# Where a fused attention kernel sums the squares of its input rows: on ScalarE beside the first projection, or on VectorE between the pieces that the projection waits for

## The chip, the cores and the metric

The kernel runs on one core of a Trainium2 chip. The metric is the device time of one execution in microseconds. Profiles are of one execution; their span runs from the first to the last instruction.

## The reference

Two transformer mixers follow each other over an input of 512 rows and 2048 columns, then a final norm. What the change touches is the beginning of the first:

```python
def rms_norm(x, g):
    y = xf * lax.rsqrt(jnp.mean(xf * xf, axis=-1, keepdims=True) + RMS_EPS)
    return y * g

h = rms_norm(x, swa_norm)                      # 512 x 2048
q, k, v, gate = jnp.split(h @ w_in, ...)       # w_in: 2048 x 4608
```

After it come window attention with sinks, an output projection, and a second layer with latent and differential attention.

## The kernel before

The kernel is one program with a hand-written order for each engine. Each engine runs its own list strictly in that order and waits on counters (semaphores) that the others raise. TensorE works through projections in chunks of 512 columns. A chunk is 16 *steps* (k = 0 to 15), one for each 128 rows of the weight; a step has 12 matmuls, for four row tiles and three products each, because both operands are split into a high and a low part: high times high, high times low, low times high. Chunk 0 holds the columns of k and v (from column 2048) and is the first work of the kernel; chunk 1 is the first with queries.

The norm's gain is applied to the transposed input `x_t` when it is split, and the division by the root of the mean square is applied only at the end of a chunk, when `evacuate` copies the four accumulators out with a scale `r_x`. So the first chunk can start before the sums of squares exist. They are needed once, at the end of chunk 0.

Around chunk 0 the engines have these lists:

- **SyncE** issues the loads in one queue: `x_t` in five pieces (`load_xt`), the weight of chunk 0 in quarters of four steps (`load_chunk(..., quads=...)`, 1 MB each), and the untransposed input `x_nat` in four tiles of 1 MB (`load_x`), which raise `s_x` by 16 each. There are two buffers for quarters, so a quarter's issue waits until GpSimd has split the last step of the quarter two before. Between the third and the fourth quarter stands the load of the first `x_nat` tile; the other three come after five small loads. Then come the quarters of chunk 1.
- **ScalarE** issues two loads itself (`gain_in`, and the first weight step into `w_raw`). Then it makes the high parts: `x_hi(k)` writes `setA_hi`, `make_hi` writes `w_hi`, three steps ahead of TensorE (`AHEAD = 3`); there are four buffers of `w_hi`, so that a high part waits for the step four before. After steps 11, 12 and 13 of its loop it squares and sums one tile of `x_nat` each, then evacuates.
- **VectorE** makes `setA_lo` from `x_t` and `setA_hi` (L2107), one for each step, all 16 in a row; TensorE's step k waits for the k-th through `s_turn_lo`. Behind them it sums the squares of the last tile of `x_nat` (L2111), waits for ScalarE's three, and forms the variance.
- **GpSimd** makes the low part of the weight (`w_lo`, L1893), three steps ahead; after the 16th it raises the variance to the power -1/2 (`root`, L1902), which gives `r_x`.

TensorE's list for chunk 0 ends with a small product for the position bias (L775). Step 0 of chunk 1 may write an accumulator when ScalarE has evacuated it.

Of the kernel before, what the change touches and what calls it, by code (L numbers as in the profile page):

```python
# [14 lines left out]
ALU = mybir.AluOpType  # L15
ACT = mybir.ActivationFunctionType
AX = mybir.AxisListType

P = 128
D = 2048  # L20
S = 512
NT = S // P
KC = D // P
CW = 512
# [10 lines left out]
BANNED = -1e30  # L35
UNITS = (GROUP // 2) * NT
X_AT = [0, 1, 2, 4, 8, 16]
X_SUMS = [11, 12, 13]
HI_FIRST = 3
EARLY = 2  # L40

# [86 lines left out]
def build(nc, a, out):  # L128
    with ExitStack() as ctx:
        at = [nc.sbuf_base + (-nc.sbuf_base) % 64]  # L130

        def place(name, shape, dt=F32, offset=None):
            size = 4
            for n in shape[1:]:
                size *= n
            if offset is None:
                offset = at[0]
                at[0] += size + (-size) % 32
            return nc.alloc_sbuf_tensor_at(name, shape, dt, offset=offset), offset

        def sb(name, shape, dt=F32):
            return place(name, shape, dt)[0]

        def over(name, shape, offset, dt=F32):
            return place(name, shape, dt, offset)[0]

        def sem(name):
            return ctx.enter_context(nc.semaphore(name))
# [6 lines left out]
        x_nat = over("x_nat", [P, NT, D], B_HI)  # L155
# [9 lines left out]
        w_raw = sb("w_raw", [P, 2, 4, CW])  # L165
        w_hi = sb("w_hi", [P, 4, CW], F32R)
        w_lo = sb("w_lo", [P, 4, CW], F32R)
        stage, STAGE = place("stage", [P, NT, CW])
        work, WORK = place("work", [P, NT, CW])
# [6 lines left out]
        half = sb("half", [P, 32])  # L176
        warmed = sb("warmed", [P, 1])
        ss_x = sb("ss_x", [P, NT])
# [144 lines left out]
        s_w0, s_w1, s_gain_in = sem("s_w0"), sem("s_w1"), sem("s_gain_in")  # L323
        s_raw = [sem(f"s_raw{i}") for i in range(2)]
        s_raw_2nd = [sem(f"s_raw_2nd{i}") for i in range(2)]
        s_hi, s_lo, s_used = sem("s_hi"), sem("s_lo"), sem("s_used")
        s_acc, s_evac = sem("s_acc"), sem("s_evac")
        s_turned, s_turn_hi, s_turn_lo = sem("s_turned"), sem("s_turn_hi"), sem("s_turn_lo")
        s_x = sem("s_x_in")
        s_xt = [sem(f"s_xt_in{j}") for j in range(len(X_AT) - 1)]  # L330
        s_small, s_ident = sem("s_small"), sem("s_ident")
        s_xsq, s_rel = sem("s_xsq"), sem("s_rel")
        s_row_ps, s_row, s_row_d = sem("s_row_ps"), sem("s_row"), sem("s_row_d")
        s_bias = sem("s_bias")
        s_var, s_root = sem("s_var"), sem("s_root")
# [56 lines left out]
        def after(eng, ins):  # L392
            link.n += 1
            ins.then_inc(s_d, 1)
            eng.wait_ge(s_d, link.base + link.n)
# [146 lines left out]
        def _(sp):  # L542
# [4 lines left out]
            def small(dst, src):  # L547
                sp.dma_start(dst, src).then_inc(s_small, 16)
# [3 lines left out]
            def next_slot():  # L552

                g = group[0]
                group[0] += 1
                free_slot(sp, g)
                return loads[g][0]

            def load_chunk(w, col, quads=(0, 1, 2, 3)):

                for rows in quads:
                    slot = next_slot()
                    sp.dma_start(w_raw[:, slot], w[:, rows, :, col:col + CW]).then_inc(s_raw[slot], 16)
# [50 lines left out]
            def load_x(t):  # L614
                sp.dma_start(x_nat[:, t], x2[t * P:(t + 1) * P]).then_inc(s_x, 16)
# [9 lines left out]
            load_xt(4)  # L625
            load_chunk(w_in, 2048, quads=(2,))
            load_x(0)
            load_chunk(w_in, 2048, quads=(3,))
            small(rel[0:32, :], a["rel_bias"])
            small(marks[:], a["t5_marks"])  # L630
            small(sinks[:], a["swa_sinks"].partition_broadcast(P))
            small(gain_qk[:, 0], a["swa_q_gain"].partition_broadcast(P))
            small(gain_qk[:, 1], a["swa_k_gain"].partition_broadcast(P))
            for t in range(1, NT):
                load_x(t)
            for i in range(4):
                load_chunk(w_in, i * CW)
            for i in range(4):
# [639 lines left out]
        def _(act):  # L1278
# [20 lines left out]
            def split_hi(c, k):  # L1299

                make_hi(B[c] + k + AHEAD)
# [40 lines left out]
            def turn_hi(b, bank, dst, gain):  # L1342
                act.wait_ge(s_turned, b + 1)
                nc.scalar.activation(dst, turn[bank][:], ACT.Copy, scale=gain).then_inc(s_turn_hi, 1)  # L1344

            act.dma_start(gain_in[:], a["swa_norm"]).then_inc(s_gain_in, 16)
            act.dma_start(w_raw[:, 0, 0], a["swa_w_in"][0:P, 2048:2048 + CW]).then_inc(s_w0, 16)
            act.sem_inc(s_evac, 4)
            act.sem_inc(MLA.free, 1)
            act.sem_inc(DIFF.free, 1)  # L1350
            act.wait_ge(s_ident, 2)
            nc.scalar.activation(warmed[:], ident[:, 0:1], ACT.Copy)
            def x_hi(k):

                if k in X_AT:
                    act.wait_ge(s_xt[X_AT.index(k)], 16)
                nc.scalar.activation(setA_hi[:, k], x_t[:, k], ACT.Copy, scale=gain_in[:, k:k + 1]).then_inc(s_turn_hi, 1)

            act.wait_ge(s_gain_in, 16)
            x_hi(0)  # L1360
            act.wait_ge(s_w0, 16)
            nc.scalar.activation(w_hi[:, 0], w_raw[:, 0, 0], ACT.Copy).then_inc(s_hi, 1)
            act.wait_ge(s_w1, 16)
            nc.scalar.activation(w_hi[:, 1], w_raw[:, 0, 1], ACT.Copy).then_inc(s_hi, 1)
            x_hi(1)
            act.wait_ge(s_raw[0], 16)
            nc.scalar.activation(w_hi[:, 2], w_raw[:, 0, 2], ACT.Copy).then_inc(s_hi, 1)
            x_hi(2)
            for k in range(KC):
                if k + AHEAD < KC:  # L1370
                    x_hi(k + AHEAD)
                split_hi(0, k)
                if k in X_SUMS:
                    t = X_SUMS.index(k)
                    act.wait_ge(s_x, 64)
                    nc.scalar.activation(x_nat[:, t], x_nat[:, t], ACT.Square,
                                         accum_out=ss_x[:, t:t + 1]).then_inc(s_xsq, 1)
            act.wait_ge(s_root, ROOT_X)
            evacuate(0, r_x)
            act.wait_ge(s_row_ps, 1)  # L1380
# [154 lines left out]
            for p in range(AHEAD + 1, PAIR + AHEAD):  # L1535
                make_hi(B["out1"] + p)
                if p in (18, 20, 22, 24):
                    t = (p - 18) // 2
# [348 lines left out]
        def _(pool):  # L1887
# [7 lines left out]
            def split_lo(c, k):  # L1895

                make_lo(B[c] + k + AHEAD)

            def root(dst, src, n, count, rows=P):

                pool.wait_ge(s_var, count)
                nc.gpsimd.tensor_tensor(dst, src, half[0:rows, 0:n], ALU.pow).then_inc(s_root, 1)  # L1902

            def block_sums(c, i, k):
# [17 lines left out]
                elif k == 14:  # L1922
# [2 lines left out]

            pool.sem_inc(s_lo, 8)
            nc.gpsimd.memset(ident[:], 0.0).then_inc(s_ident, 1)
            pool.wait_ge(s_ident, 1)
            nc.gpsimd.affine_select(out=ident[:], in_=ident[:], compare_op=ALU.not_equal, fill=1.0, base=0,
                                    pattern=[[-1, P]], channel_multiplier=1).then_inc(s_ident, 1)  # L1930
            nc.gpsimd.memset(half[:], -0.5).then_inc(s_ident, 1)
            for f in range(AHEAD):
                pool.wait_ge(s_hi, f + 1)
                nc.gpsimd.tensor_tensor(w_lo[:, f], w_raw[:, 0, f], w_hi[:, f].bitcast(F32), ALU.subtract).then_inc(s_lo, 1)
            for k in range(KC):
                split_lo(0, k)
            pool.wait_ge(s_ident, 3)
            root(r_x[:], ss_x[:], NT, ROOT_X)
            for k in range(KC):
                split_lo(1, k)  # L1940
# [79 lines left out]
            def turn_uses(A):  # L2020

                uses = sorted([(turn_time(A, h, b), 1, h) for h in range(4) for b in range(A.batches)]
                              + [(unit_time(A, u) + A.turn_after, 0, u) for u in range(NU)])
                return [max(n for n, (_, kind, h) in enumerate(uses) if kind and h == head) + 1 for head in range(4)]
# [62 lines left out]
        def _(dve):  # L2087
            V = nc.vector
# [16 lines left out]
            for b in range(KC):  # L2105
                dve.wait_ge(s_turn_hi, b + 1)
                V.scalar_tensor_tensor(setA_lo[:, b], x_t[:, b], gain_in[:, b:b + 1], setA_hi[:, b].bitcast(F32),  # L2107
                                       ALU.mult, ALU.subtract).then_inc(s_turn_lo, 1)
            dve.wait_ge(s_x, 64)
            t = NT - 1  # L2110
            after(dve, V.tensor_tensor_reduce(work[:].rearrange("p t c -> p (t c)"), x_nat[:, t], x_nat[:, t], 1.0, 0.0,  # L2111
                                              ALU.mult, ALU.add, ss_x[:, t:t + 1]))
            dve.wait_ge(s_xsq, 3)
            V.tensor_scalar(ss_x[:], ss_x[:], 1.0 / D, EPS, ALU.mult, ALU.add).then_inc(s_var, 1)


# [396 lines left out]
            for p in range(24):  # L2513
# [3 lines left out]
                if 3 <= p < 15 and p % 3 == 0:  # L2517
                    t = p // 3 - 1
# [290 lines left out]
```

## Time and profile before

| | us |
|---|---|
| median of three runs | 1616.25 (1615.15 to 1616.91) |
| the profiled execution | 1616.25 |
| its span | 1614.1 |
| TensorE busy | 1601.2, 99% of the span |
| VectorE busy | 843.7 |
| ScalarE busy | 828.9 |
| GpSimd busy | 675.8 |

The granted clock of TensorE is 0.999 of full speed in the mean. An engine's busy time says how much of the span it worked; where another engine's result is late, only the waits and the timeline show it. The profiled execution's time is 2.15 us longer than its span.

### The profile page before, as it was taken

What the parts mean: (1) busy time and instruction counts of PE and PEld (TensorE: products, weight loads), DVE (VectorE), ACT (ScalarE), POOL (GpSimd) and SP (SyncE); (2) the same over time, 40 slices, a digit from 0 to 9 for tenths busy, and PEclk for the clock granted to TensorE, in tenths of its full rate; (3) what the DMA queues carried; (4) which work ended last, traced back from release to release, by engine and by line L of the source; (5) the groups of instructions that cost most, each with busy time, mean ns of one, the idle gap of its engine ahead of it and who ended that gap; (6) DMA issues with size and microseconds to landing.
All of it is one profiled execution on the core that took longest, in us unless ns stands there. A gap on an engine that the chain in (4) does not pass through costs nothing.

```text
span 1614.1 us, 22602 instructions
## 1 busy us (share of the span) xinstructions
PE 1601.2 (99%) x8263; PEld 1337.7 (83%) x8263; DVE 843.7 (52%) x1928; ACT 828.9 (51%) x1765; POOL 675.8 (42%) x569
## 2 busy tenths in 40 slices
PE   9999999999999999999999999999999999999998
PEld 7789898888888888898888888788888888888886
DVE  5256656663123756558545451433246464877675
ACT  5456666665333454454435456444466665344561
POOL 5542433434656701676111124544444335664022
PEclk9999999999999999999999999999999999999999
DMA  8554646545778877957998948745555414624762
GB/s 341 146 157 92 157 98 177 126 111 128 184 173 195 231 223 234 294 159 194 250 258 256 252 126 274 232 129 142 150 156 118 135 56 154 142 93 140 245 241 104
DMA packets 139386, 285.44 MB, mean 177 GB/s; under 512 B 11227, under 2 KB 17820, under 8 KB 138604
## 3 DMA queue, kind: packets, MB, share of 16 engines
q1 hardware_dynamic: 85660, 164.49, 31.0%
q0 software_dynamic: 31664, 81.70, 24.3%
q10 hardware_dynamic: 21952, 37.81, 7.3%
q8 instruction: 66, 1.08, 0.3%
q14 instruction: 44, 0.36, 0.1%
HBM read 259.01 MB, written 92.06 MB: 218 GB/s over the span
## 4 chain that ended last, share of the span: by engine, by line
PE 94%; DMA 2%; issue 1%; ACT 1%; DVE 1%; POOL 1%; SPq 0%; POOLq 0%; DVEq 0%
PE acc L716 18%; PE acc L718 18%; PE acc L717 18%; PE turn L826 3%; PE turn L1174 3%; PE acc L870 2%; PE acc L869 2%; PE acc L871 2%; PE sc L871 2%; PE sc L870 2%; PE turn L870 2%; PE turn L871 2%; PE sc L869 2%; PE turn L869 2%; PE turn L814 2%; PE turn L738 1%
## 5 line engine op out<-in xcount | busy, mean ns | idle before, releaser
L1893 POOL TENSOR_TENSOR w_lo<-w_raw,w_hi 128x512 fp32r<-128x512 f32 x341 | 508.4, 1497 | 688.5 <-ACT w_hi L1297 687.4
L1297 ACT ACTIVATE w_hi<-w_raw 128x512 fp32r<-128x512 f32 x565 | 353.7, 628 | 436.7 <-PE acc L718 232.5
L716 PE MATMUL acc<-w_hi,setA_hi 128*128 128x512 f32 (+1 forms) x1076 | 429.8, 399 | 1.0 <-ACT stage L1311 0.9
L718 PE MATMUL acc<-w_hi,setA_lo 128*128 128x512 f32 (+1 forms) x1076 | 416.1, 387 | 0.0
L717 PE MATMUL acc<-w_lo,setA_hi 128*128 128x512 f32 (+1 forms) x1076 | 415.2, 386 | 0.0
L718 PEld LDWEIGHTS acc<-w_hi,setA_lo 128*128 128x128 f32 x1076 | 202.1, 188 | 41.7
L716 PEld LDWEIGHTS acc<-w_hi,setA_hi 128*128 128x128 f32 x1076 | 202.7, 188 | 34.8 <-issue 2.1
L2284 DVE TENSOR_TENSOR w_lo<-w_raw,w_hi 128x512 fp32r<-128x512 f32 x224 | 155.6, 700 | 143.6 <-ACT w_hi L1297 143.3
L717 PEld LDWEIGHTS acc<-w_lo,setA_hi 128*128 128x128 f32 x1076 | 202.9, 189 | 32.9
L1396 ACT ACTIVATE p_w<-sm,negm 128x256 f32<-128x256 f32 (+1 forms) x128 | 60.6, 474 | 57.4 <-DVE sink_d L2161 57.4
L716 PE MATMUL acc<-w_hi,setB_hi 128*128 128x512 f32 x192 | 76.8, 400 | 0.0
L718 PE MATMUL acc<-w_hi,setB_lo 128*128 128x512 f32 x192 | 75.1, 391 | 0.0
L717 PE MATMUL acc<-w_lo,setB_hi 128*128 128x512 f32 x192 | 74.8, 390 | 0.0
L1722 ACT ACTIVATE p<-sm,negm 128x144 f32<-128x144 f32 (+3 forms) x96 | 54.5, 569 | 30.5 <-DVE negm L2588 18.6
L826 PEld LDWEIGHTS turn<-vg,pT 128*128 128x128 f32 x448 | 59.9, 191 | 5.2
L826 PE MATMUL turn<-vg,pT 128*128 128x64 f32 x448 | 56.9, 267 | 0.0
L2157 DVE CUSTOM_DVE_ANT_0 sm<-sc,bias,sink_g 128x256 f32<-128x256 f32 (+1 forms) x128 | 52.5, 448 | 0.1
L2220 DVE TENSOR_TENSOR stage<-stage,work 128x2048 f32<-128x2048 f32 x7 | 16.0, 2291 | 68.0 <-ACT work L1447 62.3
L2172 DVE TENSOR_TENSOR o_nat<-turn,rden 128x128 f32<-128x128 f32 x64 | 18.7, 292 | 60.8 <-PE turn L826 60.7
L1174 PE MATMUL turn<-nat_v,pT 128*128 128x128 f32 x320 | 48.8, 283 | 0.7 <-DVE negm_far L2598 0.3
L2092 DVE SCALAR_TENSOR_TENSOR setB_lo<-turn,setB_hi 128x512 fp32r<-128x512 f32 x32 | 22.1, 691 | 50.3 <-ACT setB_hi L1344 49.7
L2581 DVE MEMSET tick<- 128x1 f32 x96 | 5.7, 59 | 81.6 <-PE sc L1113 67.4
(532 smaller groups left out, 3126.1 us busy)
## 6 DMA issues: line engine op xcount, KB each, us to landing
w_raw<-in_swa_w_in SPq DMA_DIRECT2D x35, 1024.0 KB, 7.7
w_raw<-in_w_in SPq DMA_DIRECT2D x32, 1024.0 KB, 5.5
w_raw<-sum_out SPq DMA_DIRECT2D x64, 256.0 KB, 4.2
sum_k<-in_w_in POOLq DMA_DIRECT2D x24, 512.0 KB, 6.7
sum_out<-in_swa_w_out POOLq DMA_DIRECT2D x24, 512.0 KB, 7.7
sum_v<-in_w_in POOLq DMA_DIRECT2D x24, 512.0 KB, 8.1
w_raw<-in_w_in SPq DMA_DIRECT2D x48, 256.0 KB, 5.3
sum_out<-in_w_out POOLq DMA_DIRECT2D x24, 512.0 KB, 6.7
```

The lines of the kernel that those rows point to most:

```text
L716: mm(acc[t][:, 0:cols], hi[:, kc, rows], wh, start=(k == 0), stop=False)
L717: mm(acc[t][:, 0:cols], hi[:, kc, rows], wl, start=False, stop=False)
L718: last = mm(acc[t][:, 0:cols], lo[:, kc, rows], wh, start=False, stop=(k == K - 1))
L826: last = mm(o_ps[:, h * HD:(h + 1) * HD], pT[:, u % 2, 2 * h + c], vg[:, j - 1 + c], start=(c == (1 if j == 0 else 0)), stop=(c == 1))
L869: mm(dst, hi, wh, start=start, stop=False)
L870: mm(dst, hi, wl, start=False, stop=False)
L871: last = mm(dst, lo, wh, start=False, stop=stop)
L1174: mm(dst, pT2[:, u % 2, b * P:(b + 1) * P], nat_v[:, buf, b], start=(b == 0), stop=False)
L1297: nc.scalar.activation(w_at(f)[0], raw_of(f), ACT.Copy).then_inc(done, 1)
L1396: nc.scalar.activation(p_w[:, u % 2, h, first:], sm[:, u % 2, h, first:], ACT.Exp, bias=negm[:, u % 2, h:h + 1], scale=-1.0, accum_out=den ...
L1893: nc.gpsimd.tensor_tensor(lo, raw_of(f), hi.bitcast(F32), ALU.subtract).then_inc(s_lo, 1)
L2284: V.tensor_tensor(lo, raw_of(f), hi.bitcast(F32), ALU.subtract).then_inc(s_wlo, 1)
```

## The change

The sums of squares of all four tiles go to VectorE. They stand inside its loop over the 16 steps, behind the low parts of steps 8, 10, 12 and 14; ahead of the first one stands a wait for all four tiles of `x_nat`. ScalarE's three squares are gone. The loads of the `x_nat` tiles are interleaved with the fourth quarter of the weight and put ahead of the small loads. At the very start ScalarE issues the first weight step before the gain, and makes `w_hi` of step 0 before `setA_hi` of step 0. The constant `half` has a semaphore of its own and is written before the second half of the identity matrix.

```diff
-X_SUMS = [11, 12, 13]
+X_SUMS = [8, 10, 12, 14]
@@ SyncE
             load_chunk(w_in, 2048, quads=(2,))
             load_x(0)
+            load_x(1)
             load_chunk(w_in, 2048, quads=(3,))
+            load_x(2)
+            load_x(3)
             small(rel[0:32, :], a["rel_bias"])
...
             small(gain_qk[:, 1], a["swa_k_gain"].partition_broadcast(P))
-            for t in range(1, NT):
-                load_x(t)
             for i in range(4):
                 load_chunk(w_in, i * CW)
@@ ScalarE
+            act.dma_start(w_raw[:, 0, 0], a["swa_w_in"][0:P, 2048:2048 + CW]).then_inc(s_w0, 16)
             act.dma_start(gain_in[:], a["swa_norm"]).then_inc(s_gain_in, 16)
-            act.dma_start(w_raw[:, 0, 0], a["swa_w_in"][0:P, 2048:2048 + CW]).then_inc(s_w0, 16)
...
             nc.scalar.activation(warmed[:], ident[:, 0:1], ACT.Copy)
+            act.wait_ge(s_w0, 16)
+            nc.scalar.activation(w_hi[:, 0], w_raw[:, 0, 0], ACT.Copy).then_inc(s_hi, 1)
...
             x_hi(0)
-            act.wait_ge(s_w0, 16)
-            nc.scalar.activation(w_hi[:, 0], w_raw[:, 0, 0], ACT.Copy).then_inc(s_hi, 1)
...
                 split_hi(0, k)
-                if k in X_SUMS:
-                    t = X_SUMS.index(k)
-                    act.wait_ge(s_x, 64)
-                    nc.scalar.activation(x_nat[:, t], x_nat[:, t], ACT.Square,
-                                         accum_out=ss_x[:, t:t + 1]).then_inc(s_xsq, 1)
@@ GpSimd
             nc.gpsimd.memset(ident[:], 0.0).then_inc(s_ident, 1)
+            nc.gpsimd.memset(half[:], -0.5).then_inc(s_half, 1)
             pool.wait_ge(s_ident, 1)
...
-            nc.gpsimd.memset(half[:], -0.5).then_inc(s_ident, 1)
...
-            pool.wait_ge(s_ident, 3)
+            pool.wait_ge(s_half, 1)
             root(r_x[:], ss_x[:], NT, ROOT_X)
@@ VectorE, inside "for b in range(KC)"
                                        ALU.mult, ALU.subtract).then_inc(s_turn_lo, 1)
-            dve.wait_ge(s_x, 64)
-            t = NT - 1
-            after(dve, V.tensor_tensor_reduce(work[:].rearrange("p t c -> p (t c)"), x_nat[:, t], x_nat[:, t], 1.0, 0.0,
-                                              ALU.mult, ALU.add, ss_x[:, t:t + 1]))
-            dve.wait_ge(s_xsq, 3)
+                if b in X_SUMS:
+                    t = X_SUMS.index(b)
+                    if t == 0:
+                        dve.wait_ge(s_x, 64)
+                    after(dve, V.tensor_tensor_reduce(work[:].rearrange("p t c -> p (t c)"), x_nat[:, t], x_nat[:, t], 1.0, 0.0,
+                                                      ALU.mult, ALU.add, ss_x[:, t:t + 1]))
             V.tensor_scalar(ss_x[:], ss_x[:], 1.0 / D, EPS, ALU.mult, ALU.add).then_inc(s_var, 1)
```

## Rows read from the trace of the kernel before

**Rows 1.** The page: the span, and busy time of each engine with its share.

```profile
span 1614.1 us, 22602 instructions
PE 1601.2 (99%) x8263; PEld 1337.7 (83%) x8263; DVE 843.7 (52%) x1928; ACT 828.9 (51%) x1765; POOL 675.8 (42%) x569
```

**Rows 2.** Timeline of TensorE: start, duration, line, operation; idle before and its releaser.

```profile
6.38 1.20 PE L760 MATMUL acc<-w_hi,setA_hi 128*128 128x512 f32 x4 [1.37 <-ACT w_hi L1362]
...
30.99 0.39 PE L716 MATMUL acc<-w_hi,setA_hi 128*128 128x512 f32 x1
...
49.81 0.39 PE L718 MATMUL acc<-w_hi,setA_lo 128*128 128x512 f32 x1
50.12 0.83 PE L775 MATMUL sc<-marks,rel 33*32 33x384 f32 x2
51.90 0.47 PE L716 MATMUL acc<-w_hi,setA_hi 128*128 128x512 f32 x1 [0.94 <-ACT stage L1311]
```

**Rows 3.** Timeline of VectorE around its loop over the steps of chunk 0.

```profile
20.90 1.39 DVE L2107 SCALAR_TENSOR_TENSOR setA_lo<-x_t,gain_in,setA_hi 128x512 fp32r<-128x512 f32 x1 [0.31 <-ACT setA_hi L1357]
...
42.05 0.75 DVE L2107 SCALAR_TENSOR_TENSOR setA_lo<-x_t,gain_in,setA_hi 128x512 fp32r<-128x512 f32 x1 [5.58 <-ACT setA_hi L1357]
42.71 3.39 DVE L2111 CUSTOM_DVE_ANT_0 work<-x_nat 128x2048 f32<-128x2048 f32 x1
```

**Rows 4.** Timeline of SyncE: when it issues the loads in question.

```profile
12.84 1.11 SPq L615 DMA_DIRECT2D x_nat<-in_x  x1
21.77 0.37 SPq L563 DMA_DIRECT2D w_raw<-in_swa_w_in  x1
...
25.28 1.38 SPq L615 DMA_DIRECT2D x_nat<-in_x  x3
```

**Rows 5.** Loads issued at 12.84, 21.77, 25.28, 26.23 and 30.50: us to landing last.

```profile
x_nat<-in_x SPq DMA_DIRECT2D x1, 1024.0 KB, 13.9
...
w_raw<-in_swa_w_in SPq DMA_DIRECT2D x1, 1024.0 KB, 7.5
...
x_nat<-in_x SPq DMA_DIRECT2D x1, 1024.0 KB, 8.5
...
DMA to landing us min/median/max: 13.1/13.1/13.1
...
w_raw<-in_swa_w_in SPq DMA_DIRECT2D x1, 1024.0 KB, 11.4
```

**Rows 6.** Timeline of ScalarE: first weight part, first square, first evacuations.

```profile
5.69 0.63 ACT L1362 ACTIVATE w_hi<-w_raw 128x512 fp32r<-128x512 f32 x1 [1.25 <-DMA w_raw<-in_swa_w_in]
...
39.40 1.92 ACT L1376 ACTIVATE x_nat<-x_nat 128x2048 f32<-128x2048 f32 x1 [2.13 <-DMA x_nat<-in_x]
...
51.07 2.42 ACT L1311 ACTIVATE stage<-acc,r_x 128x512 f32<-128x512 f32 x4 [2.92 <-POOL r_x L1902]
```

**Rows 7.** Timeline of GpSimd in the second half of chunk 0.

```profile
37.34 1.29 POOL L1893 TENSOR_TENSOR w_lo<-w_raw,w_hi 128x512 fp32r<-128x512 f32 x1 [1.43 <-ACT w_hi L1297]
42.61 1.34 POOL L1893 TENSOR_TENSOR w_lo<-w_raw,w_hi 128x512 fp32r<-128x512 f32 x1 [3.98 <-ACT w_hi L1297]
45.03 2.22 POOL L1893 TENSOR_TENSOR w_lo<-w_raw,w_hi 128x512 fp32r<-128x512 f32 x1 [1.08 <-ACT w_hi L1297]
...
50.00 1.03 POOL L1902 TENSOR_TENSOR r_x<-ss_x,half 128x4 f32<-128x4 f32 x1
```

**Rows 8.** Groups of VectorE by form: busy, mean ns; the same custom reduction elsewhere.

```profile
L2588 DVE CUSTOM_DVE_ANT_0 sm<-sc,mask 128x528 f32<-128x528 f32 x8 | 5.7, 707 | 0.1
...
L2588 DVE CUSTOM_DVE_ANT_0 sm<-sc,mask 128x144 f32<-128x144 f32 x8 | 2.5, 308 | 0.0
```

**Rows 9.** TensorE's last matmul; then windows: length, busy by engine, PEclk, DMA share, GB/s.

```profile
1606.25 0.39 PE L1265 MATMUL turn<-we_hi,setB_lo 128*128 128x512 f32 x1
...
1608.00:1610.00 2.00, 0.00 (x0) 0.00 (x0) 1.19 (x3) 1.15 (x3) 0.54 (x1) 0.96 0.00 0
1610.00:1612.00 2.00, 0.00 (x0) 0.00 (x0) 0.12 (x1) 0.12 (x1) 0.00 (x0) 0.50 0.86 302
```

More of the change, by code:

```diff
@@ L331, in build @@
         s_small, s_ident = sem("s_small"), sem("s_ident")
-        s_xsq, s_rel = sem("s_xsq"), sem("s_rel")
+        s_half, s_rel = sem("s_half"), sem("s_rel")
         s_row_ps, s_row, s_row_d = sem("s_row_ps"), sem("s_row"), sem("s_row_d")
```

## The prediction

> **What bounds the kernel now.** I read the page first: TensorE is busy 1601.2 of 1614.1 us [rows 1], so whatever holds TensorE moves the end, and whatever does not hold it is free. Its idle time is 12.9 us. The timeline says where: the first matmul of chunk 0 starts at 6.38 with 1.37 idle before it (the rest of the start is warm-up work), 0.94 stands before step 0 of chunk 1 at 51.90 [rows 2], and the last matmul ends at 1606.25 + 0.39 = 1606.64, which leaves 7.5 us of tail [rows 9]. The other waits together are small change. So the most this change can win is the 0.94 and a piece of the start; the 0.2% (3.2 us) that a measurement of this kernel can tell from no change is out of its reach. What it can lose is not bounded like that, so the reading goes to what TensorE waits for in chunk 0, and to the loads of `x_nat`.
>
> Steps of chunk 0 run without a gap: step 9 begins at 30.99 [rows 2], the last matmul of step 15 starts at 49.81, and these seven steps of 12 matmuls are 84, so one matmul takes (49.81 - 30.99) / 83 = 0.2267 us and a step 2.72 us.
>
> **Part one, the added wait.** VectorE runs its list in order. The new list is: low part of step 8, wait for all four `x_nat` tiles, reduction, low part of step 9. TensorE's step 9 needs that low part. Before, `setA_lo` of step 8 was made at 20.90 [rows 3], long ahead; the wait for `x_nat` stood behind all 16 low parts, where nothing of chunk 0 was queued behind it. Now the low parts of steps 9 to 15 are.
>
> When is the last tile there? Landing is issue plus the time to landing [rows 4, 5]: first tile 12.84 + 13.9 = 26.7; fourth weight quarter 21.77 + 7.5 = 29.3; second tile 25.28 + 8.5 = 33.8; fourth tile 26.23 + 13.1 = 39.4, where ScalarE indeed ends its wait [rows 6]; then chunk 1's first quarter, 30.50 + 11.4 = 41.9. Each is 1 MB of one queue, and they land in order: 2.6 us apart where only one follows another (26.7 to 29.3, 39.4 to 41.9: 2.5), and (39.4 - 33.8) / 2 = 2.8 between the second, third and fourth tile. From 29.3 to 33.8 it is 4.5, because the five small loads lie between: they cost 1.9.
>
> The new order after the first tile is second tile, fourth quarter, third tile, fourth tile, then the small loads. The second tile is issued straight behind the first, the last two behind the quarter at 21.77, by about 23, so the queue does not run dry. The fourth tile lands at 26.7 + 4 x 2.6 = 37.1. Lower bound: 4 x 2.5 gives 36.7. Upper bound: the 39.4 of now. The fourth quarter slips to 31.9, which is hidden (TensorE will not reach step 12 before 48), and so do the small loads, which L775 needs after 59.
>
> Then the reduction. Its one row says 3.39 us, but a GpSimd operation was running when it was issued: 42.61 + 1.34 = 43.95 [rows 7], and the reduction ended at 42.71 + 3.39 = 46.10 [rows 3], 2.15 later. GpSimd's next one, started at 45.03, took 2.22 instead of about 1.3 and ended 1.15 after the reduction. The two take turns. The same custom operation elsewhere costs 308 ns for 144 elements and 707 for 528 [rows 8], 1.04 ns an element, which makes 308 + 1904 x 1.04 = 2.29 us for 2048. While TensorE stands, GpSimd has nothing to do (its `w_lo` of step 12 is made, that of 13 needs step 9 done). I take 2.2, bounds 2.15 and 3.39.
>
> By the Trainium skill ("SBUF — State Buffer", SBUF: two separate sides) a VectorE operation with two SBUF inputs and a GpSimd operation that reads SBUF exclude each other for whole instructions. The trace agrees with it: 2.15 behind GpSimd's end. By the opposite reading, all 3.39 work, the sum below would be 1.2 higher.
>
> Behind it come 0.75 for the low part when VectorE is alone [rows 3] and some 0.3 for three hand-overs (load to VectorE, reduction to its successor, VectorE to TensorE; w_hi ends at 5.69 + 0.63 = 6.32 and TensorE starts at 6.38 [rows 2, 6], so 0.06 to 0.1 each). Step 9 starts at 37.1 + 2.2 + 0.75 + 0.3 = 40.35 instead of 30.99: **+9.4** (bounds: 36.7 and 2.15 give +8.9; 39.4 and 3.39 give +12.8).
>
> **Part two, the clock.** TensorE would stand for 9.4 us, which it does nowhere in the trace but in the tail. There the granted clock is 0.96 in the stretch 1608 to 1610 and 0.50 from 1610 on [rows 9], that is 1.2 in place of 2.4 GHz, after the last matmul at 1606.64. So the clock will probably fall in the gap, and step 9 begins at the low level. No row shows how it comes back. At half speed a step would take 5.44, so the price lies between 0 and one step's extra 2.7; I take the middle, **+1.4**. By the Trainium skill ("TensorE: Matmul & The Clock Gate", The HAM clock gate) the throttled clock is the default and activity releases it, which speaks for a price above 0; no row here shows the rise.
>
> **Part three, the later sums.** The pairs behind it (two low parts and a reduction) cost VectorE 2 x 0.75 + 2.2 + 0.2 for hand-overs = 3.9 us against 2 x 2.72 = 5.44 of TensorE. With GpSimd in between each low part is about 1.3 (1.39 at 20.90 [rows 3]) and a reduction up to 3.39: 2 x 1.39 + 3.39 = 6.2 at most, late by 0.75 a pair for three pairs. I take 0 and keep 2.2 as the bound.
>
> **Part four, the end of chunk 0.** ScalarE loses three squares of 1.92. These made the high parts behind them late, and through them GpSimd, which reached `root` at 50.00; the evacuation began at 51.07 [rows 6, 7] and TensorE resumed 0.83 later. Without them the last `w_lo` follows step 14. In steady state `w_lo` ends 2.20 after the step it waits for (step 10 ends at 30.99 + 2 x 2.72 = 36.43, `w_lo` at 37.34 + 1.29 = 38.63). Step 14 ended at 47.31; 47.31 + 2.20 + 1.03 for the root + 0.04 + 0.83 = 51.41 in place of 51.90: **-0.5** (bounds 0 and -0.94). VectorE's four sums are ready before the root: the last begins behind the low part of step 14, about 18 us after the loads, and step 14 of TensorE ends some 20 after them.
>
> **Part five, the start.** The first weight step is issued 0.48 earlier (the length of one issue), but `setA_hi` now follows `w_hi`: from the landing to TensorE's start it takes two ScalarE operations, 2 x 0.63 + 0.06 = 1.3, where it took 0.69 (5.69 to 6.38 [rows 2, 6]), so the first matmul moves by +0.1 (if the load lands as much earlier as it is issued) to +0.6. This is worth **0**, because steps 0 to 8 end before a gap whose end the loads set. If that gap did not exist it would count. The move of `half` is 0.12 of GpSimd before anything waits for it: 0.
>
> **The sum.** 9.4 + 1.4 - 0.5 = +10.3. The profiled execution took 1616.25, as the median did, so 1626.55; I say 1626.5, and a span near 1624.4. Nothing later gives it back, since of TensorE's 12.9 idle us 7.5 are the tail, 0.94 the wait at 51.90 and 1.37 that at 6.38, which leaves 3.1 at most for everything else.
>
> **The rivals.**
>
> *A, the sum as above*, with the clock falling: 1626.5, its own range 1624.5 to 1629. Chance 0.62.
>
> *B, the stall without the clock.* The gap is there, but TensorE's clock stays or returns at once: 1616.25 + 9.4 - 0.5 = 1625.1. For it: no stretch with matmuls in this trace has a low clock. Against: the tail. Chance 0.15.
>
> *C, more than the one stall.* Fourth tile as late as now (+2.3), or the reductions at 3.39 and the pairs late (+1.2 and +2.2 at most). For it: the 2.8 a tile in today's last two, and the taking of turns. With one half of it, +3: 1629.5. Chance 0.17.
>
> *D, the wait is covered* and no slower than before. It needs the four tiles by 30.99 - 0.75 - 2.2 - 0.3 = 27.7, which is the point from which it decides; then only part four counts and the start: 1616.25 - 0.5 = 1615.8. For it: the tiles are issued earlier. Against: at 2.6 us a megabyte only the first tile is there at 27.7. Chance 0.05. That it comes out over 0.2% faster I give 0.01, the rest.
>
> B, C and A all are slower by over 3.2 us, so slower 0.94, same 0.05, faster 0.01. The range takes A and B whole and most of C: 1623.5 (bounds +8.9, no clock, -0.94: 1624.2, a little under for the spread of the runs) to 1630.5.
>
> **What would show it.** In the profile after, VectorE's first reduction should begin at about 37, not behind a ScalarE wait but behind the loads of `x_nat`; TensorE should show one idle stretch of about 9.4 us before a matmul of step 9, released by `setA_lo`; the granted clock in the next 3 us should be near 0.5; the wait of 0.94 before chunk 1 should shrink to about 0.45. Wrong would be: `x_nat` landing before 28; a busy TensorE through step 9; or a longer stall because the fourth tile lands as late as now.

## The result

The changed kernel takes 1625.98 us (median of 5 runs, 1624.83 to 1627.23) against 1616.91 for the kernel before, measured beside it (5 runs, 1615.15 to 1618.87): ratio 1.0056, 95% interval 1.0042 to 1.0072. It is 9.1 us slower, against a forecast of 10.3 more and 1626.5 in all. The forecast added its sum to 1616.25, and the median beside it is now 0.66 higher, so the time came out 0.5 off while the difference is 1.2 off. The profiled execution took 1625.0 with a span of 1623.2.

The page of the changed kernel, span and busy time:

```profile
span 1623.2 us, 22605 instructions
PE 1602.8 (99%) x8263; PEld 1337.8 (82%) x8263; DVE 847.2 (52%) x1934; ACT 823.0 (51%) x1759; POOL 675.4 (42%) x569
```

TensorE has the same 8263 matmuls and is busy 1.6 us longer, while the span grew by 9.1: most of the loss is idle time. The timeline of TensorE, changed kernel:

```profile
6.17 1.17 PE L761 MATMUL acc<-w_hi,setA_hi 128*128 128x512 f32 x4 [1.17 <-issue]
...
30.57 0.39 PE L719 MATMUL acc<-w_hi,setA_lo 128*128 128x512 f32 x1
39.81 0.80 PE L717 MATMUL acc<-w_hi,setA_hi 128*128 128x512 f32 x1 [8.86 <-DVE setA_lo L2103]
...
42.10 0.63 PE L719 MATMUL acc<-w_hi,setA_lo 128*128 128x512 f32 x1
42.53 0.50 PE L717 MATMUL acc<-w_hi,setA_hi 128*128 128x512 f32 x1
...
44.03 0.40 PE L717 MATMUL acc<-w_hi,setA_hi 128*128 128x512 f32 x1
...
60.46 0.83 PE L776 MATMUL sc<-marks,rel 33*32 33x384 f32 x2
61.71 0.47 PE L717 MATMUL acc<-w_hi,setA_hi 128*128 128x512 f32 x1 [0.41 <-ACT stage L1312]
```

Read beside [rows 2]: step 9 starts at 39.81 in place of 30.99, behind 8.86 idle us that VectorE's low part ends. Step 10 starts at 44.03, so step 9 took 4.22 and not 2.72; its matmuls are 0.43 apart until 42.53. Before chunk 1 the wait is 0.41 where it was 0.94. VectorE's timeline shows what stood in front of that low part:

```profile
20.72 1.47 DVE L2103 SCALAR_TENSOR_TENSOR setA_lo<-x_t,gain_in,setA_hi 128x512 fp32r<-128x512 f32 x1 [0.23 <-ACT setA_hi L1360]
36.66 2.29 DVE L2109 CUSTOM_DVE_ANT_0 work<-x_nat 128x2048 f32<-128x2048 f32 x1 [14.48 <-DMA x_nat<-in_x]
38.88 0.08 DVE L2109 DVE_READ_ACCUMULATOR2_ANT ss_x<- 128x1 f32 x1
39.00 1.42 DVE L2103 SCALAR_TENSOR_TENSOR setA_lo<-x_t,gain_in,setA_hi 128x512 fp32r<-128x512 f32 x2
```

VectorE stands for 14.48 us on the loads of `x_nat` with the low part of step 9 queued behind. The windows of the same kernel (length, busy time by engine, granted clock, DMA share, GB/s) give TensorE's clock:

```profile
34.00:35.00 1.00, 0.00 (x0) 0.00 (x0) 0.00 (x0) 0.00 (x0) 0.00 (x0) 1.00 0.88 243
35.00:36.00 1.00, 0.00 (x0) 0.00 (x0) 0.00 (x0) 0.00 (x0) 0.00 (x0) 0.96 0.66 237
36.00:37.00 1.00, 0.00 (x0) 0.00 (x0) 0.34 (x1) 0.00 (x0) 0.00 (x0) 0.50 0.96 357
...
42.00:43.00 1.00, 1.00 (x4) 0.78 (x4) 0.96 (x3) 0.00 (x0) 0.00 (x0) 0.62 0.00 0
43.00:44.00 1.00, 1.00 (x6) 0.81 (x5) 1.00 (x3) 0.00 (x0) 0.00 (x0) 1.00 0.00 0
```

It falls to 0.50 (1.2 GHz) in the gap, stays there through the first matmuls of step 9, rises in the course of the window from 42 to 43 and is at 1.00 (2.4 GHz) from 43 on.

### The profile page after: what moved, and what is told of

Same layout as the page of the kernel before. It is cut to its first block, busy times and chain, and to the rows that moved or that the text cites. A ratio compares the mean times of both kernels' runs of the same rounds, so it can differ in the third digit from the quotient of the medians.

```text
span 1623.2 us, 22605 instructions
## 1 busy us (share of the span) xinstructions
PE 1602.8 (99%) x8263; PEld 1337.8 (82%) x8263; DVE 847.2 (52%) x1934; ACT 823.0 (51%) x1759; POOL 675.4 (42%) x569
## 4 chain that ended last, share of the span: by engine, by line
PE 95%; DMA 2%; issue 1%; POOL 1%; DVE 0%; ACT 0%; SPq 0%; POOLq 0%; DVEq 0%
PE acc L717 18%; PE acc L719 18%; PE acc L718 18%; PE turn L827 3%; PE turn L1175 3%; PE acc L871 2%; PE acc L870 2%; PE acc L872 2%; PE sc L872 2%; PE sc L871 2%; PE turn L872 2%; PE turn L871 2%; PE sc L870 2%; PE turn L870 2%; PE turn L815 2%; PE turn L739 1%
```

## The experiments

Each is compared with the kernel before on the same chip, whose median there was 1616.9 to 1617.4. The changed kernel was not run again beside them: differences from its 1625.98 are between runs made at different times.

**A wait for each tile.** `s_wl[t]` are four semaphores that the program otherwise raises only near its end; their later waits became 32.

```diff
-                sp.dma_start(x_nat[:, t], ...).then_inc(s_x, 16)
+                sp.dma_start(x_nat[:, t], ...).then_inc(s_wl[t], 16)
...
-                    if t == 0:
-                        dve.wait_ge(s_x, 64)
+                    dve.wait_ge(s_wl[t], 16)
```

> The changed kernel with a wait for each tile of x_nat in place of the one wait for all four; sums, places and load order as changed. Theory (the wait for the last tile is what TensorE pays for): tiles land near 25.1, 29.0, 34.0 and 36.6, each is summed about when its place in the list comes, the low part of step 9 is there at 28.2 and TensorE needs it at 30.8: no idle time before step 9, no fall of the clock, about 10.3 us less than the changed kernel, 1615.6. Rival (four reductions of 2.3 us between the low parts are too much for VectorE in chunk 0): a gap stays before one of the steps 9, 11, 13 or 15 and the time stays above 1620.

Measured: 1616.67 (11 runs), ratio to the kernel before 0.9995 (0.9986 to 1.0004), 1.1 over the expected 1615.6. All of the loss is gone, with the same four reductions on VectorE, in the same places of its list and with the same load order. Its VectorE timeline:

```profile
26.86 2.52 DVE L2107 CUSTOM_DVE_ANT_0 work<-x_nat 128x2048 f32<-128x2048 f32 x1 [4.22 <-DMA x_nat<-in_x]
...
29.42 2.32 DVE L2102 SCALAR_TENSOR_TENSOR setA_lo<-x_t,gain_in,setA_hi 128x512 fp32r<-128x512 f32 x2
31.66 3.38 DVE L2107 CUSTOM_DVE_ANT_0 work<-x_nat 128x2048 f32<-128x2048 f32 x1
```

The first reduction waits 4.22 for one tile and not 14.48 for four. TensorE has no wait between two steps of chunk 0. The landing of 25.1 in the expectation is missed by 1.7 without harm. In this profile the first matmuls ran slowly (see below), so step 9 was due 2.3 late; the profile of `tile_root_warm` below, whose start is at full speed, shows no wait there either.

**The wait alone**, put into the kernel before:

```diff
                                        ALU.mult, ALU.subtract).then_inc(s_turn_lo, 1)
+                if b == 8:
+                    dve.wait_ge(s_x, 64)
             dve.wait_ge(s_x, 64)
```

> The kernel before with nothing but VectorE's wait for all four tiles added behind the low part of step 8; no sum is moved, load order as before. Theory: the last tile lands at 39.4, the low part of step 9 follows 0.75 later, TensorE starts step 9 at 40.3 in place of 31.0 and runs most of it at the low clock: +9.3 and +1.5, 1627 to 1628. Rival (the sums on VectorE are the cost, not the wait): no more than 1 us over the kernel before.

Measured: 1626.19 (4 runs), ratio 1.0055 (1.0041 to 1.0069), the changed kernel's 1.0056 to within the intervals. It is 0.8 under the expected 1627 to 1628: the last tile was there at 38.5 and not at 39.4. VectorE and TensorE, this kernel:

```profile
38.52 3.40 DVE L2107 SCALAR_TENSOR_TENSOR setA_lo<-x_t,gain_in,setA_hi 128x512 fp32r<-128x512 f32 x5 [16.16 <-DMA x_nat<-in_x]
...
39.33 0.80 PE L716 MATMUL acc<-w_hi,setA_hi 128*128 128x512 f32 x1 [8.60 <-DVE setA_lo L2107]
```

One wait, which adds no work to any engine, makes the whole loss. The rival that the sums are the cost falls.

**The sums behind the loop**, the wait left where it is:

```diff
-                if b in X_SUMS:
+                if b == X_SUMS[0]:
+                    dve.wait_ge(s_x, 64)
+            for t in range(NT):
+                after(dve, V.tensor_tensor_reduce(...))
```

> The changed kernel with the wait left behind step 8 but all four reductions moved behind step 15. Theory: the gap before step 9 ends one reduction earlier (2.3 us), so 1623.7, and up to 1 us of it is given back where the four sums at the end make the root late. Rival (reductions are the cost): close to the kernel before.

Measured: 1629.62 (4 runs), ratio 1.0077 (1.0062 to 1.0092): 5 to 6 us over what was expected. The gap did shrink, but the end of the chunk gave back far more than the "up to 1 us". Timelines of VectorE, GpSimd and TensorE:

```profile
50.28 3.26 DVE L2108 CUSTOM_DVE_ANT_0 work<-x_nat 128x2048 f32<-128x2048 f32 x1
...
53.58 3.26 DVE L2108 CUSTOM_DVE_ANT_0 work<-x_nat 128x2048 f32<-128x2048 f32 x1
...
51.69 9.57 POOL L1889 TENSOR_TENSOR w_lo<-w_raw,w_hi 128x512 fp32r<-128x512 f32 x3 [0.31 <-ACT w_hi L1298]
...
37.28 0.80 PE L717 MATMUL acc<-w_hi,setA_hi 128*128 128x512 f32 x1 [6.27 <-DVE setA_lo L2103]
...
63.33 0.76 PE L717 MATMUL acc<-w_hi,setA_hi 128*128 128x512 f32 x1 [3.53 <-ACT stage L1312]
```

The gap is 6.27, 2.6 shorter. But the reductions run against GpSimd's `w_lo`: the last three take 3.26 each in place of 2.29, and three `w_lo` take 9.57 in place of 3 x 1.29. The variance is late, the wait before chunk 1 is 3.53, and in the windows around it the clock falls a second time:

```profile
62.00:63.00 1.00, 0.00 (x0) 0.00 (x0) 0.00 (x0) 0.50 (x1) 0.47 (x1) 0.99 0.00 0
63.00:64.00 1.00, 0.67 (x2) 0.60 (x3) 0.00 (x0) 1.00 (x3) 0.00 (x0) 0.50 0.00 0
```

Against the changed kernel that is -2.6 for the gap, +1.1 for a longer low clock in and after step 9 (it is back only at 42.5, 5.2 us after 37.28, where the changed kernel had 2.6), +3.1 for the wait before chunk 1 and +1.5 for the seven matmuls there at 0.43: +3.1, where the spans differ by 1626.5 - 1623.2 = 3.3. The spread of the sums over the steps is what keeps them free in the changed kernel.

**Matmuls in the gap**, first 16 and then 34 more of the warm-up kind. They write a scratch bank that nobody reads.

```diff
+                if k == 9:
+                    for n in range(FILL):
+                        mm(sc[1][:, 0:P], ident[:], ident[:], start=True, stop=True)
                 pe.wait_ge(s_turn_lo, k + 1 + EARLY)
```

> The changed kernel with 16 more of the warm-up matmuls in TensorE's list ahead of its wait for the low part of step 9 (0.476 us each, 7.6 us, so they end near 38.4, ahead of the 39.8 at which step 9 starts). They write a scratch bank that nobody reads. Theory (the clock costs 1.5 us on top of the gap): the granted clock stays at full speed, step 9 takes 2.7 us in place of 4.2 and the kernel 1.5 us less than the changed one, 1624.4. Rival (the slow first matmuls are not the clock's, or cost nothing in the end): 1626 as the changed kernel, or more.

Measured: 1625.5 (5 runs), ratio 1.0052 (1.004 to 1.0065). It did not test what it was made for. The 16 were over in half the time reckoned with, and 5.15 idle us stayed, in which the clock still fell, only later, and it also came back later. TensorE of this kernel, around the extra matmuls (32 records for 16 of them) and step 9, and two windows:

```profile
30.74 3.73 PE L773 MATMUL sc<-ident 128*128 128x128 f32 x32
39.63 0.79 PE L718 MATMUL acc<-w_hi,setA_hi 128*128 128x512 f32 x1 [5.15 <-DVE setA_lo L2107]
...
44.91 0.63 PE L718 MATMUL acc<-w_hi,setA_hi 128*128 128x512 f32 x1
...
45.74 0.39 PE L720 MATMUL acc<-w_hi,setA_lo 128*128 128x512 f32 x1
...
38.00:40.00 2.00, 0.37 (x1) 0.38 (x2) 1.96 (x4) 0.00 (x0) 0.00 (x0) 0.72 0.21 81
...
44.00:46.00 2.00, 2.00 (x7) 1.53 (x6) 2.00 (x1) 0.85 (x2) 0.14 (x1) 0.57 0.00 0
```

From 39.63 to 45.74 it did 14 matmuls, which take 3.17 at full speed: the low clock cost 2.9 in the profiled execution. That one took 1626.23; three of the five runs lie at 1625.2 to 1625.5, and what the clock cost in those no profile shows. The run with 34:

> As filled_gap, with 34 extra warm-up matmuls in place of 16. In filled_gap they ran at 0.233 us each, so 16 ended at 34.5 and left 5.15 idle; 34 take 7.9 us and end near 38.7, 1 us before step 9. Theory (the clock falls only after TensorE has stood for some us, and its fall costs 1.5 us and more): the granted clock stays at 1.00, step 9 takes 2.7 us, 1.5 us less than in the changed kernel, and the time is 1624 to 1624.5 where the kernel before is at 1616.9. Rival (slow first matmuls in step 9 have another cause than the clock): step 9 still takes 4 us or more, and the time is that of the changed kernel.

Measured: 1624.1 (5 runs, 1623.77 to 1624.97), ratio 1.0045 (1.0033 to 1.0058). Timeline of TensorE and two windows:

```profile
32.51 7.75 PE L773 MATMUL sc<-ident 128*128 128x128 f32 x68
40.40 0.50 PE L718 MATMUL acc<-w_hi,setA_hi 128*128 128x512 f32 x1
40.73 0.39 PE L719 MATMUL acc<-w_lo,setA_hi 128*128 128x512 f32 x1
...
39.00:40.00 1.00, 1.00 (x12) 1.00 (x10) 0.96 (x3) 0.00 (x0) 0.00 (x0) 1.00 0.12 45
40.00:41.00 1.00, 0.87 (x6) 0.59 (x5) 1.00 (x3) 0.00 (x0) 0.00 (x0) 1.00 0.04 14
```

The clock stays at 1.00, step 9 runs from 40.40 at 0.23 a matmul, and the kernel is 1.9 us below the changed one, in which step 9 took 1.5 longer than a step at full speed. The intervals of the two ratios overlap, so it is the profiled step more than the median that decides: with TensorE busy up to 0.14 us before it, step 9 is not slow. So the fall is the cause of the slow step 9, and its price is real. The gap itself can't be won back so; the matmuls in it are waste.

**The loads in another order**, the fourth weight quarter behind all tiles:

```diff
             load_x(1)
-            load_chunk(w_in, 2048, quads=(3,))
             load_x(2)
             load_x(3)
+            load_chunk(w_in, 2048, quads=(3,))
```

> The changed kernel with the third and fourth tile of x_nat issued ahead of the fourth weight quarter. Theory (the landing of the fourth tile sets the end of the gap): it lands one megabyte, 2.5 us, earlier, near 34.1, the gap before step 9 ends 2.5 earlier, and the time is 1623.5. The fourth quarter lands near 36.6 and TensorE does not need it before 46. Rival (the end of the gap is set by something else, or the late quarter costs as much): 1626.

Measured: 1623.79 (4 runs), ratio 1.0039 (1.0024 to 1.0054). VectorE's wait and the start of step 9:

```profile
34.11 2.29 DVE L2109 CUSTOM_DVE_ANT_0 work<-x_nat 128x2048 f32<-128x2048 f32 x1 [11.70 <-DMA x_nat<-in_x]
...
37.25 0.50 PE L717 MATMUL acc<-w_hi,setA_hi 128*128 128x512 f32 x1 [4.09 <-DVE setA_lo L2103]
```

The fourth tile lands 2.55 earlier and step 9 starts 2.56 earlier: the landing sets the gap's end, one to one. The gap reads 4.09 because in this profile step 9 was due only at 33.0: the start of chunk 0 had run at the low clock, see below. The clock fell here too, but only at 38.3, a microsecond into step 9:

```profile
38.30:38.60 0.30, 0.30 (x2) 0.29 (x1) 0.30 (x1) 0.00 (x0) 0.30 (x1) 0.51 0.38 143
```

**The wait further down**, same load order:

```diff
-X_SUMS = [8, 10, 12, 14]
+X_SUMS = [12, 13, 14, 15]
```

> The changed kernel with the reductions behind the steps 12, 13, 14 and 15 in place of 8, 10, 12 and 14; the one wait for all four tiles stays, load order as changed. Theory (only where the wait stands matters): the wait ends at 36.7, the low part of step 13 is there at 39.8 and TensorE needs it at 41.7, so no gap before step 13; three reductions close together may make step 15 up to 0.5 late and the root some 0.5: 1616 to 1617. Rival (four sums on VectorE are too much, or the load order costs by itself): over 1619.

Measured: 1620.31 (10 runs), ratio 1.002 (1.0011 to 1.0029): 3 to 4 us over the theory's number and on the rival's side of 1619. No gap stands before step 13, so the place of the wait is most of it. But of the reductions close together the last two meet GpSimd and take 3.38 and 3.37:

```profile
45.36 3.38 DVE L2109 CUSTOM_DVE_ANT_0 work<-x_nat 128x2048 f32<-128x2048 f32 x1
...
50.48 0.50 PE L717 MATMUL acc<-w_hi,setA_hi 128*128 128x512 f32 x1 [1.24 <-DVE setA_lo L2103]
55.98 0.47 PE L717 MATMUL acc<-w_hi,setA_hi 128*128 128x512 f32 x1 [1.71 <-ACT stage L1312]
```

Step 15 waits 1.24 and chunk 1 waits 1.71, 1.3 more than in the changed kernel: 2.5 us, which is most of the 3.1 by which this kernel is over its own kernel before. So both theories hold something: at this spacing the sums do cost. The load order does not, since `tile_waits` has the same one and is back at the time of the kernel before.

**The start alone**, in the kernel before:

```diff
+            act.dma_start(w_raw[:, 0, 0], ...).then_inc(s_w0, 16)
             act.dma_start(gain_in[:], a["swa_norm"]).then_inc(s_gain_in, 16)
-            act.dma_start(w_raw[:, 0, 0], ...).then_inc(s_w0, 16)
...
+            act.wait_ge(s_w0, 16)
+            nc.scalar.activation(w_hi[:, 0], w_raw[:, 0, 0], ACT.Copy).then_inc(s_hi, 1)
...
             x_hi(0)
-            act.wait_ge(s_w0, 16)
-            nc.scalar.activation(w_hi[:, 0], w_raw[:, 0, 0], ACT.Copy).then_inc(s_hi, 1)
```

> The kernel before with the start alone as changed: ScalarE issues the first weight step ahead of the gain and makes the high part of the weight first. Theory: the first matmul moves from 6.38 to about 6.17 as in the changed kernel, and all behind it by 0.2: 1616.0 to 1616.9, not to be told from the kernel before by its median. Rival (the start moves the loads so that a later step is late): over 1618.

Measured: 1616.23 (11 runs), ratio 0.9997 (0.9988 to 1.0005): not to be told from the kernel before. The first matmul is at 6.03. Its wait before chunk 1 was 0.42 although ScalarE squares three tiles here too; the tiles had landed a microsecond earlier, as ScalarE's first square shows, at 38.36 where [rows 6] has 39.40:

```profile
38.36 1.92 ACT L1376 ACTIVATE x_nat<-x_nat 128x2048 f32<-128x2048 f32 x1 [1.13 <-DMA x_nat<-in_x]
```

**The best of them.** To the waits by tile is added an earlier root, and then two more warm-up matmuls (`WARM` 7 to 9).

```diff
             for k in range(KC):
                 split_lo(0, k)
-            pool.wait_ge(s_half, 1)
-            root(r_x[:], ss_x[:], NT, ROOT_X)
+                if k == 13:
+                    pool.wait_ge(s_half, 1)
+                    root(r_x[:], ss_x[:], NT, ROOT_X)
```

> The changed kernel with a wait for each tile, and GpSimd raising the variance to the power -1/2 two low parts earlier, so that the scale is there before TensorE ends chunk 0. Theory (what is left of the wait before chunk 1 is the root behind the last low part): the gap of 0.41 before step 0 of chunk 1 shrinks to 0.1 or less: 1615.2, some 10.7 below the changed kernel and 1 to 1.5 below the kernel before. Rival (the accumulators' copies themselves set it): the gap of 0.41 stays.

Measured: 1616.08 (11 runs, 1615.55 to 1616.82), ratio 0.9994 (0.9985 to 1.0003). The wait before chunk 1 is gone from the waits of TensorE. The time is 0.9 over the expected 1615.2 and 1.2 below the kernel before, within the noise of the ratio. Its first matmuls:

```profile
6.16 2.04 PE L760 MATMUL acc<-w_hi,setA_hi 128*128 128x512 f32 x4 [1.15 <-issue]
8.00 1.64 PE L763 MATMUL acc<-w_hi,setA_lo 128*128 128x512 f32 x4
```

Four matmuls take 2.04 where [rows 2] has 1.20: the low clock, at the start. Against it:

```diff
-WARM = 7
+WARM = 9
```

> tile_waits_root with 9 warm-up matmuls in place of 7. In four of ten profiles the first 8 to 11 matmuls of chunk 0 run at 0.43 us apiece, half speed, which costs 1.3 to 2.3 us. Theory (TensorE's 1.2 us of idle time between the warm-up and the first step decides whether the clock is up): the warm-up ends near 6.0 at most, the first four matmuls take 1.2 us and the median is 0.5 to 1 us below tile_waits_root's, about 1.5 below the kernel before. Rival (the low start comes from where the clock stands when the kernel begins, whatever the warm-up): the first four matmuls can still take 2.0, and the median does not move.

Measured: 1614.64 (11 runs, 1614.21 to 1615.06), ratio 0.9987 (0.9978 to 0.9996). This beats both kernels: 0.13% below the kernel before and 11.3 us below the changed one. The prediction held a difference under 0.2% for out of reach of a measurement; eleven runs that lie within 0.9 us of each other resolve this one. It is also more than was expected: 1.4 below `tile_waits_root`, where 0.5 to 1 was forecast. Timeline of TensorE:

```profile
1.68 4.18 PE L750 MATMUL sc<-ident 128*128 128x128 f32 x18 [1.68 <-POOL ident L1925]
6.21 1.15 PE L760 MATMUL acc<-w_hi,setA_hi 128*128 128x512 f32 x4 [0.35 <-issue]
```

The idle time between warm-up and step 0 is 0.35, the first four take 1.15. Is it the warm-up alone? The kernel before with `WARM = 9`:

> The kernel before with 9 warm-up matmuls in place of 7 and nothing else. Theory (most of tile_root_warm's 2.3 us below the kernel before is the clock at the start): the first four matmuls of chunk 0 take 1.2 us in every profile, the median is 1 to 1.5 us below the kernel before, and its runs lie closer together. Rival (the 2.3 us are the waits by tile and the earlier root): the median does not move.

Measured: 1615.99 (11 runs, 1615.43 to 1618.27), ratio 0.9995 (0.9986 to 1.0004): 1.1 below the kernel before beside it, as expected, but within the noise of the ratio. The start is at full speed, but the runs did not close up: nine lie at 1615.4 to 1616.5, two at 1618.1 and 1618.3. The profiled one is of the two, and TensorE's timeline and windows say why:

```profile
50.45 0.83 PE L775 MATMUL sc<-marks,rel 33*32 33x384 f32 x2
52.62 0.47 PE L716 MATMUL acc<-w_hi,setA_hi 128*128 128x512 f32 x1 [1.33 <-ACT stage L1311]
...
55.16 0.63 PE L718 MATMUL acc<-w_hi,setA_lo 128*128 128x512 f32 x1
...
54.00:55.00 1.00, 1.00 (x4) 0.81 (x3) 0.69 (x1) 0.54 (x2) 0.00 (x0) 0.50 0.00 0
```

Here the small product and a wait of 1.33 stood before chunk 1, and the clock fell a microsecond after TensorE had resumed. It also waited 0.53 for GpSimd before step 4. So this kernel has two places where the low clock was seen in some executions, the start and the end of chunk 0. The two kernels with nine warm-up matmuls start at full speed in their one profile each, the earlier root takes the wait at the end away, and only both together bring the median down by 2.3 us and the runs within 0.9 of each other. Two profiles do not show that nine warm-up matmuls always suffice, and whether it is the shorter idle time or the longer warm-up that helps was not separated. That both places explain the whole spread of the kernel before is inferred; only profiled runs show their clock.

## Why the prediction was right

**The added wait** (9.4 forecast, 8.8 measured) was the right step for the right reason. The fourth tile was there at 36.66 against 37.1. The first landed at 12.89 + 12.2 = 25.1 and not at 26.7, the second 3.8 behind it, at 28.9, and the next three megabytes 2.5 to 2.7 apart, as forecast. The trace of before has such a long interval too, 3.9 between the third weight quarter (22.8) and the first tile; here it lies one megabyte further on. From the third quarter to the fourth tile it is 14.1 us, where the prediction's numbers make 14.3, so the sum did not hang on it; what makes the long interval, no run shows. The reduction took 2.29 with GpSimd idle. That is the prediction's own figure from the slope of [rows 8]; its 2.2 and its lower bound of 2.15 were a little short, and the 3.39 of [rows 3] did hold 1.1 of waiting for GpSimd. From the landing to step 9 it took 3.15, against 3.25. The wait alone, by tile, and with the loads reordered settle it three ways.

**The clock** (1.4 forecast between 0 and 2.7; 1.5 measured) is right in size here, partly by luck. Taking the middle between two bounds has no mechanism behind it, and the upper one was no bound: the fall cost 2.9 with 16 matmuls in the gap, since the low clock lasted longer than one step. The median of 1625.98 lies between this sum (1626.5) and rival B (1625.1, the stall without the clock), so the time alone would not have decided between them; the windows and the gap filled with 34 matmuls do, against B.

**The later sums** (0 forecast, bound 2.2) cost nothing as placed: steps 10 to 15 and the small product took 60.46 - 44.03 = 16.43, as before (16.41, from 30.99 + 2.72 to 50.12 in [rows 2]). That the bound was real shows where they are bunched. The prediction put the last sum about 18 us behind the loads; it began 12.9 behind them, at 49.59, well ahead of the root.

**The end of chunk 0** (-0.5 forecast) measured -0.53: from the small product to step 0 it is 1.25 in place of 1.78. The chain behind step 14 ran as worked out, but the kernel before is not always late by this much: the squares on ScalarE make the root late only as far as the tiles land late. In the three profiles with all squares and no gap the first square began at 38.36, 39.40 and 40.12 (start alone, before, nine warm-up matmuls alone), and the wait was 0.42, 0.94 and 1.33. So the gain depends on the execution of the kernel before that it is taken from; that it came out at the forecast owes something to forecasting from that same profile.

**The start** (0) is right, but its working was not: the first matmul was to move by +0.1 to +0.6 and came 0.2 earlier. ScalarE, changed kernel:

```profile
4.43 0.63 ACT L1355 ACTIVATE w_hi<-w_raw 128x512 fp32r<-128x512 f32 x1 [1.05 <-DMA w_raw<-in_swa_w_in]
5.35 0.72 ACT L1360 ACTIVATE setA_hi<-x_t,gain_in 128x512 fp32r<-128x512 f32 x1 [0.29 <-DMA gain_in<-in_swa_norm]
```

The weight was there 1.26 earlier (5.69 in [rows 6]) and not 0.48, and `setA_hi` then waited for the gain, so the two operations did not follow each other from the landing of the weight. The gap absorbed the shift, as argued.

Together 8.82 + 1.50 + 0.02 - 0.53 = 9.81 at the start of chunk 1 (51.90 to 61.71). The spans differ by 9.1. The other 0.7 lies in later waits of TensorE, 1.0 us of them in the profile before and 0.3 in the one after, which also differ from run to run between kernels of equal code there.

Rival D, the covered wait, was given the right point of decision: 27.7. With one wait for each tile the first reduction starts at 26.9 (25.2 in the profile of `tile_root_warm`) and no step is late.

## What to carry to other kernels

In an in-order list a wait costs what is queued behind it, and not what it guards: before a wait is moved ahead of work that a busy engine needs, compare the landing time of its last transfer with the time at which that work is due. One counter for several transfers waits for the last of them; where they are used one by one, give each its own. And an idle stretch of TensorE has a second price behind it, in the clock, so short gaps at seams (here the start and the end of a chunk) may be worth closing together.

## What the runs showed of the hardware

- The low clock at the start, unseen by the clock column. In five of the eleven profiles with seven warm-up matmuls the first matmuls of chunk 0 ran some 0.43 us apart, a loss of 1.4 to 2.3 us, while the granted clock of those stretches reads 1.00. The warm-up matmuls took 3.33 us for seven (0.476 each) at the start, in the kernel before too, and 3.73 for sixteen (0.233 each) in the middle of the kernel: by this spacing the first ones run at the low level. The prediction's sentence that no stretch with matmuls has a low clock was read from the column and is wrong; the spacing of the matmuls shows it.
- A custom reduction with both inputs in SBUF and GpSimd's subtraction exclude each other: 2.29 alone, 3.26 to 3.39 together, and GpSimd's 1.29 becomes 2.2 to 3.2. By the Trainium skill ("SBUF — State Buffer", SBUF: two separate sides) the two hold a port pair by turns for whole instructions; these runs agree.
- Behind each of the six waits of 3.5 to 8.9 us, in five profiles, the clock fell. Behind the small product and a wait of 1.33 it fell in one profile, 1 us after TensorE had resumed; behind the same product and a wait of 1.71 (`sums_late`) it stayed at 1.00. So the length of the wait alone does not say whether it falls; what else decides, no run shows. The price where it was counted was 1.5 to 2.9 us a fall.
